# Four modulation chunks taken from TensorE to VectorE, beside the second layer's gate jobs

## The reference

```
mod = silu(c) @ w_mod[l] + b_mod[l]          # c is one row; w_mod is 1024 x 6144
sh1, sc1, gt1, sh2, sc2, gt2 = split(mod, 6)
h = rms_norm(x, g_norm1[l]) * (1.0 + sc1) + sh1
...
x = x + gt1 * mix
```

## Time and profile before

| | us |
|---|---|
| median of 3 runs | 1231.23 (1230.91 to 1231.29) |
| the profiled execution: its time | 1228.16 |
| its span, first to last instruction | 1226.4 |
| PE busy | 1177.4 (96%) |
| DVE busy | 511.6 (42%) |
| ACT busy | 302.6 (25%) |
| POOL busy | 23.0 (2%) |

### The profile page before, as it was taken

The page is one execution under the profiler, slowest core; times in us unless marked ns, Lnnn a source line. Parts: engine busy times, 40 slices in busy tenths (PEclk is TensorE's granted clock), DMA queues, the critical chain, the costliest instruction groups (busy, mean ns, idle before and its releaser), DMA issues.

```text
span 1226.4 us, 15316 instructions
## 1 busy us (share of the span) xinstructions
PE 1177.4 (96%) x6080; PEld 700.1 (57%) x6080; DVE 511.6 (42%) x1220; ACT 302.6 (25%) x703; POOL 23.0 (2%) x33
## 2 busy tenths in 40 slices
PE   4999999989999999999999898999999999999996
PEld 2446876654478888667885586444444444444442
DVE  3323329962356440692599633122222222222223
ACT  0000128970150001571421333111111111111112
POOL 0000000000000001120000000000000000000000
PEclk9999999999999999999999698999999999999999
DMA  9852219003251325466455666999999999999990
GB/s 345 306 206 69 69 35 377 3 27 132 109 214 69 126 81 156 128 178 219 150 215 184 237 257 274 401 427 427 429 428 429 428 428 428 428 428 428 429 415 39
DMA packets 82325, 311.40 MB, mean 254 GB/s; under 512 B 18129, under 2 KB 19228, under 8 KB 69466
## 3 DMA queue, kind: packets, MB, share of 16 engines
q1 hardware_dynamic: 78672, 309.56, 64.3%
q10 hardware_dynamic: 3386, 0.86, 0.3%
q0 software_dynamic: 208, 0.17, 0.1%
HBM read 309.40 MB, written 1.18 MB: 253 GB/s over the span
## 4 chain that ended last, share of the span: by engine, by line
PE 85%; DVE 10%; DMA 2%; ACT 2%; issue 1%; SPq 1%; DVEq 0%; ACTq 0%
PE ps L1164 18%; PE ps L831 11%; PE ps L1196 9%; PE ps L912 9%; PE ps L1130 5%; PE ps L1142 5%; DVE G L2014 4%; PE ps L746 3%; PE ps L876 3%; PE ps L862 3%; PE ps L691 3%; PE ps L849 3%; PE ps L782 2%; PE ps L1014 2%; PE ps L990 2%; DMA ring<-in_a_w_in 2%
## 5 line engine op out<-in xcount | busy, mean ns | idle before, releaser
L1164 PE MATMUL ps<-ring,prob 128*64 128x512 f32 x704 | 188.1, 592 | 1.2 <-issue 1.2
L1164 PEld LDWEIGHTS ps<-ring,prob 128*64 128x64 f32 x704 | 61.8, 137 | 100.3 <-issue 100.3
L912 PE MATMUL ps<-U,ring 128*128 128x256 f32 (+1 forms) x384 | 111.6, 451 | 0.0
L2179 DVE TENSOR_TENSOR prob<-ps,prob 128x512 f32<-128x512 f32 x16 | 17.2, 1076 | 193.7 <-PE ps L1164 193.7
L912 PEld LDWEIGHTS ps<-U,ring 128*128 128x128 f32 x384 | 72.5, 190 | 37.3 <-issue 31.0
L1196 PE MATMUL ps<-ring,prob 128*64 128x512 f32 x352 | 78.0, 595 | 0.0
L1164 PE MATMUL ps<-K,prob 128*64 128x512 f32 x160 | 70.3, 592 | 0.0
L746 PE MATMUL ps<-U,ring 128*128 128x256 f32 (+1 forms) x224 | 70.0, 471 | 0.0
L1130 PEld LDWEIGHTS ps<-bias,U 128*128 128x128 f32 x512 | 60.2, 197 | 13.4 <-issue 13.4
L1304 ACT ACTIVATE prob<-ps,soft 128x512 f32<-128x512 f32 (+2 forms) x112 | 64.2, 592 | 9.1 <-DVE soft L1700 7.1
L1130 PE MATMUL ps<-bias,U 128*128 128x128 f32 x512 | 63.2, 283 | 1.1 <-DVE bias L2140 1.1
(11 more groups left out here) (358 smaller groups left out, 1723.7 us busy)
## 6 DMA issues: line engine op xcount, KB each, us to landing
ring<-in_w_exp_gate SPq DMA_DIRECT2D x22, 2048.0 KB, 18.5
ring<-in_w_exp_up SPq DMA_DIRECT2D x20, 2048.0 KB, 16.8
ring<-in_w_exp_down SPq DMA_DIRECT2D x20, 2048.0 KB, 19.8
ring<-in_w_ada SPq DMA_DIRECT2D x12, 2048.0 KB, 16.3
ring<-in_w_mod SPq DMA_DIRECT2D x12, 2048.0 KB, 8.8
ring<-in_b_w_in SPq DMA_DIRECT2D x8, 2048.0 KB, 8.8
ring<-in_a_w_in SPq DMA_DIRECT2D x5, 2048.0 KB, 18.1
ring<-in_w_in SPq DMA_DIRECT2D x5, 2048.0 KB, 10.0
```

Source lines behind the costliest of these rows:

```text
L912: last = mm(ps[:, m % 4, 0:width], slot(n)[:, k, (m % 4) * P:(m % 4 + 1) * P], src[:, k, 0:width], start=(k == 0), stop=(k == KT - 1))
L1164: last = mm(ps[x * CAP:(x + 1) * CAP, 2 + i, :], xg[:, k, x * CAP:(x + 1) * CAP], chunk(n, 2 * i + x, turn)[0][:, k, :], start=(k == 0), s ...
```

## The change

A new stage, mod_v, holds chunks 2 to 5 of w_mod. The DVE weighs them after it has joined the last products of layer b's input: for each chunk one multiplication and seven multiply-adds over 128x512, each into the same sum, in tile `prob`. PE sums a chunk over the partitions with 8 instructions of one column (`fold_sums`), before gate jobs 3, 5 and 7 and after the last one. One DVE instruction then takes all 16 columns. `stream`, `mod_rows`, `fold` and `take_mod2` for these chunks are gone from their three places. In the plan the first two of mod_v go before b_in's chunks 6 and 7, the others behind them; mod_a keeps chunks 0 and 1. The lines that call `load_bias` are unchanged.

```
-            ("b_in", "b_w_in", 0, range(8)),
-            ("mod_a", "w_mod_2", 0, range(4)), ("b_out", "b_w_out", 0, range(2)), ("mod_a", "w_mod_2", 0, (4, 5)),
+            ("b_in", "b_w_in", 0, range(6)), ("mod_v", "w_mod_2", 0, (2, 3)), ("b_in", "b_w_in", 0, (6, 7)),
+            ("mod_v", "w_mod_2", 0, (4, 5)), ("mod_a", "w_mod_2", 0, (0, 1)), ("b_out", "b_w_out", 0, range(2)),
...
+        vsum = prob[:, 1:3, :].rearrange("p a (b n) -> p (a b) n", b=2)
+        st["mod_v"] = tk["b_in", "dve"]
...
+                    if L == "b" and n == 0:
+                        pe.wait_ge(mod_ok, 5)
...
+            def fold_sums(i):
+                pe.wait_ge(tk["b_in", "dve"], dve_count("b_in", ("mod", i)))
+                for m in range(4):
+                    last = mm(ps[:, 5, 4 * i + m:4 * i + m + 1], vsum[:, i, m * P:(m + 1) * P], meanm[:, 0:1],
+                              start=True, stop=True)
+                last.then_inc(col_done, 1)
...
+                if m in (3, 5, 7):
+                    fold_sums(m // 2 - 1)
...
+            fold_sums(3)
...
-            modulation("mod_a", range(2, 4), 2, 1, (4, 5), 6)
...
-            stream("mod_a", 4, 6)
...
-            fold("mod_a", 4, 2, 1, 7)
-            stream("mod_a", 5, 6)
-            fold("mod_a", 5, 2, 1, 7)
...
-            mod_rows("mod_a", range(2, 4), (4, 5))
...
-            mod_rows("mod_a", (4,), (6,))
...
-            mod_rows("mod_a", (5,), (6,))
...
+            def weigh_chunk(i):
+                n = PLACE["mod_v"][i]
+                dve.wait_ge(full[n % SLOTS], 16 * (n // SLOTS + 1))
+                w, to = slot(n), vsum[:, i, :]
+                step(v.tensor_scalar(to, w[:, 0, :], sil[:, 0, 2:3], None, ALU.mult))
+                for k in range(1, KT):
+                    settle()
+                    ins = v.scalar_tensor_tensor(to, w[:, k, :], sil[:, k, 2:3], to, ALU.mult, ALU.add)
...
+            for i in range(4):
+                weigh_chunk(i)
+            dve.wait_ge(col_done, CHUNKS["mod_v"] + 4)
+            v.scalar_tensor_tensor(mod2[:, 8:24], ps[:, 5, 0:16], float(D), vec[:, VAT["b_mod_2"] + 8:VAT["b_mod_2"] + 24],
+                                   ALU.mult, ALU.add).then_inc(mod_ok, 1)
...
-                if k == 8:
-                    take_mod2(CHUNKS["mod_a"] + 6, 16, 16, 24, 7)
```

More of the change, by code:

```diff
@@ L192 @@
     + unit_events(3) + unit_events(4) + [(5, "s1")] + unit_events(5) + [(5, "s2"), (5, "s4")]
-    + unit_events(6) + unit_events(7)}
+    + unit_events(6) + unit_events(7) + [("mod", i) for i in range(4)]}
 def dve_count(stage, event):
@@ L392, in build @@
         row_ok, col_done = sem("row_ok"), sem("col_done")
-        CHUNKS = {"ada0": 0, "ada1": 6, "mod_a": 12, "mod_b": 18}
+        CHUNKS = {"ada0": 0, "ada1": 6, "mod_v": 12, "mod_a": 16, "mod_b": 18}
+        ROWS = {"ada0": 0, "ada1": 6, "mod_a": 12, "mod_b": 14}
+        vsum = prob[:, 1:3, :].rearrange("p a (b n) -> p (a b) n", b=2)
+        st["mod_v"] = tk["b_in", "dve"]
         sil_zero = sem("sil_zero")
@@ L411, in build @@
             used[s] = [c + 1 for c in range(6)]
+        used["mod_v"] = [dve_count("b_in", ("mod", i)) for i in range(4)]
         def slot(n):
@@ L695, in fold @@
             def fold(stage, c, v0, nv, bank):
-                pe.wait_ge(row_ok, CHUNKS[stage] + c + 1)
+                pe.wait_ge(row_ok, ROWS[stage] + c + 1)
                 row = modrow(stage, c)
@@ L999, in _ @@
             pe.wait_ge(at["o"], past["b", "o"] + len(UN["b"]) - 1)
-            modulation("mod_a", range(2, 4), 2, 1, (4, 5), 6)
             pe.wait_ge(at["o"], past["b", "o"] + len(UN["b"]))
             out_proj("b_out", oT, S)
-            pe.wait_ge(mod_ok, 5)
+            pe.wait_ge(mod_ok, 6)
             def raw_c(i):
@@ L1107, in _ @@
             for i, c in enumerate((4, 5)):
-                pe.wait_ge(row_ok, CHUNKS["mod_b"] + c + 1)
+                pe.wait_ge(row_ok, ROWS["mod_b"] + c + 1)
                 mm(ps[:, 1 + i, :], foldw, modrow("mod_b", c), start=True, stop=False)
@@ L1904, in _ @@
             join_products("b_in", 7)
+            def weigh_chunk(i):
[6 more added lines that the diff above has]
+                    ins = v.scalar_tensor_tensor(to, w[:, k, :], sil[:, k, 2:3], to, ALU.mult, ALU.add)
+                    if k < KT - 1:
+                        step(ins)
+                    else:
+                        ins.then_inc(tk["b_in", "dve"], 1)
+            for i in range(4):
[3 more added lines that the diff above has]
+                                   ALU.mult, ALU.add).then_inc(mod_ok, 1)
             attention("b", bias_b)
@@ L1917, in gains @@
                 settle()
-            take_mod2(CHUNKS["mod_a"] + 4, S, 0, 16, 6)
-            dve.wait_ge(mod_ok, 5)
+            take_mod2(CHUNKS["mod_a"] + 2, S, 0, 8, 6)
+            dve.wait_ge(mod_ok, 6)
             gains(0, "g_norm1_2", 8)
```

## The result

The changed kernel takes 1237.7 us in the median of 6 runs (1236.9 to 1242.3); the kernel before took 1231.3 on the same chip (1230.4 to 1234.0). The ratio is 1.0057, with a 95% interval of 1.0039 to 1.0074: 5 to 9 us slower. Forecast was slower, 1241 (1233 to 1247). The profiled execution has a span of 1235.6, 9.2 more than the one of before.

A forecast was written before the change was run, and what follows sets the result against it. PE makes up 85% of the chain, with the DVE's convolution bounding 624.25 to 673.2. The terms 12.0 + 0.5 - 4.9 - 0.4 - 0.1 + 2.8 give +9.9 us on 1231.23, so 1241.1 us, range 1233 to 1247.

The forecast's parts named there:

- gate jobs, then last fold: Before attention b: three folds inside the gate jobs and a fourth after them start attention b 3.3 us later.
- POOL's fifth mask: In attention b: POOL gets the biases of heads 4 and 5 at 523.5 instead of 510.15.
- end of attention b: From unit 4 on the 43.8 us stand, so the end moves 12.0 us later, plus 0.5 for TensorE's clock.
- folds in attention c: 24 fold instructions, 2.77 us, run at half clock after a PE pause near the convolution's end: +2.8 us (0 to 5).
- Weighing: DVE beside the gate jobs: multiply-adds of about 0.75 us, 24 us for four chunks, done at 496; cost on the path 0.
- The queue: SP's ring after the gate jobs: biases issued behind three 2 MB loads instead of one, and unable to overtake them.
- the term of 12.0: In attention b: unit 4's bias is added 12.0 us later, at 525.3; 8.8 of this is stall from SP's queue.
- Rival 2: At SP's queue: small loads mix with the 2 MB ones, so no stall; 1229.1 or 1231.9 us; chance 0.10.
- Rival 3: In attention b: TensorE's clock does not come back after the stall, up to +37 us, near 1275; chance 0.03.
- Rival 1: The stall comes, but the clock in attention c falls where it falls now: +7.1, 1238.3 us; chance 0.22.
- Between attention b and b_out: b_out starts right behind attention b's last output, without two streams and their folds: gain 4.9 us (4.5 to 5.4).
- A pause anywhere is paid later: On PE: any pause, even beside the bound, lowers TensorE's clock, so PE time turned into a pause is no gain.

The follow-up runs named there:

- Experiment 2: Kernel before the change, with only the biases of heads 4 to 15 issued two chunks later and nothing weighed on the DVE: 1241.4 us, ratio 1.0087.
- experiment 1: Changed kernel, with the biases of heads 4 to 15 issued directly behind b_out's second chunk, one 2 MB load ahead: 1229.6 us, ratio 0.9985 to the kernel before.
- experiment 5: Changed kernel, with the four 96 KB bias loads of heads 4 and 5 issued by ScalarE from another queue: 1241.7 us, ratio 1.0082 to the kernel before.
- experiment 3: As experiment 1, plus five unused 512-column matmuls on PE before attention c's scores of unit 2: 1226.2 us, ratio 0.9966 to the kernel before.
- experiment 4: As experiment 1, but only chunks 2 and 3 weighed by the DVE, chunks 4 and 5 streamed on PE again: 1224.1 us, ratio 0.9942 to the kernel before.
- experiment 7: As experiment 1, but each chunk weighed twice on the DVE: 1246.9 us profiled, 1250.7 to 1256.4 in three others; ratio 1.0198 to the kernel before.

## Why the prediction was right

The direction and the mechanism were right in each step that the prediction took; the sum was +9.9 and the stages show +8.0. Corrected by the 1.2 us that the execution was late:

| step | predicted | measured |
|---|---|---|
| DVE done | 496 (494 to 502) | 497.6 |
| wait of PE for the sums | 0 | 0 |
| gate jobs, then last fold | + 3.3 | + 2.9 |
| POOL's fifth mask | 523.5 | 523.0 |
| unit 4's bias | 525.3 | 524.8 |
| end of attention b | + 12.5 (12.0 and 0.5 for the clock) | + 12.5 (11.6 and 0.9) |
| b_out starts | + 7.6 | + 7.4 |
| convolution done | + 7.1 | + 6.8 |
| folds in attention c | + 2.8 (half clock) | + 2.4; the stage + 3.1 |
| the rest | 0 | - 1.9 |

- *Weighing.* Multiply-adds of 0.75 were right once alone (5.48 for seven, 0.78 each); beside POOL's four masks (476 to 482) seven took 6.45 and 5.99, and three of the masks 0.97 to 1.20 where they are 0.86 alone. Experiment 2 shows that the weighing had no part in the stall.
- *The queue.* Experiments 1 and 2, one line each way, give -8.9 and +10.7: the 8.8 of stall within the term of 12.0 was the price, and it came from counting loads ahead of the biases and not from any engine's busy time. That the end of attention b came out at +12.5 to the tenth is luck: the bias came 0.4 earlier than foretold, and what followed it took 0.4 longer. One part of the picture was off without changing the number: SP itself stood 4.1 us in issuing c_in's second chunk.
- *Rival 2* (small loads slip between large ones) is refuted here, and by experiment 5 for another queue too, where head 4 gained 4.7 us and head 5 nothing. *Rival 3* too: the clock is back at 533. *Rival 1* gives 1238.3, which is nearer to the 1237.7 than the forecast's own 1241.1, so the time alone would have spoken for it; the 5.21 us of the folds rule it out, and experiment 3 shows the pause to be the cause.
- *Between attention b and b_out.* 4.9 foretold; 5.0 measured in experiments 1 and 4 (first scores to b_out, 63.0 to 58.0).
- *A pause anywhere is paid later* was too strong: after the wait of 2.20 us in experiment 7 the granted clock stayed at 1, where the earlier trace rows have it at 0.5 after 2.42 us.
- *What I did not foresee* is the end: the 3.4 us for which the DVE stands idle in the kernel before are 0.9 in the changed one, it seems by accident of its code's place. That took off 2.5 us; behind attention c as a whole it is 1.9, since 0.6 was lost elsewhere there. The forecast of 1241.1 is 3.4 us above the measured 1237.7, and the 1.9 is the larger part of this; the other 1.5 is smaller than the spread of either kernel's runs.

## What to carry to other kernels

A hook that says "just before this chunk's slot comes free" moves when the plan is reordered: count again what stands ahead of every small load that shares the queue, and issue small urgent loads before large patient ones. Take work from the bound engine only where it is on the path: two of these four chunks gave the 5.0 us in front of b_out; the other two gained 1.1 more up to the end of the convolution (experiment 1 against 4), and cost 1.8 of folds and 3.9 in attention c, where their pause brought the clock down early. And compare stages, not ends, where an unrelated wait at the end can differ between two programs by 2.5 us, a good part of an effect like this one.

## What the runs showed of the hardware

- 96 KB loads in packets of about 240 bytes land 6.7 us after their issue behind one 2 MB load, 16.0 behind three, and 10.4 (head 4) when issued from another queue beside the same three; head 5, whose last part was issued 1.9 later, was there at 528.3, after 15.
- After a pause of 4.0 us of PE beside attention c the granted clock went from 1 to 0.5, within 1 us of its end; five matmuls that nobody needs, 4.6 us of PE, put the fall off until after the folds. After a wait of 2.20 us in experiment 7 it stayed at 1.
- The DVE's first instruction behind a jump had 0.9 or 3.2 to 3.4 us of idle time before it, it seems by the place of the code behind the jump; eight instructions some 750 us ahead of it made the difference, in one execution.
- POOL's additions and the DVE's multiply-adds were slower beside each other: a mean of 0.92 us against 0.78 for a multiply-add in a chain of seven, 0.97 to 1.20 against 0.86 for three of four masks.
